# The order of the three partial products inside one half of a weight unit, in a one-core fp32 decoder step

## The reference, cut to what matters

```
z    = x @ w_in + b_in                      # 2048 x 6656: q, k, v, pooling input, two gates
d    = multi-scale causal pooling of z's pooling part
pool = (d @ w_pool[g]) * pool_scale         # 4 groups, 256 x 512 each
attn = sliding-window attention @ w_attn_br # 1024 x 2048
m    = sigmoid(g_pool) * pool + sigmoid(g_attn) * attn
h    = layer_norm(ALPHA * x + m @ w_out)    # 2048 x 2048
q    = h @ w_query                          # 2048 x 2048, then key scores and two top-16
a    = h @ peer_u.T                         # 16384 experts x 2048, computed for all experts here
y    = layer_norm(ALPHA * h + (gelu(a) * gate) @ peer_v)   # 16384 x 2048
```

## Time and profile before

| | |
|---|---|
| device time, median of 3 runs | 2319.65 us (2319.39 to 2319.66) |
| span of the profiled execution, first to last instruction | 2318.2 us |
| matmuls, and weight loads | 17575 and 17575 |
| TensorE busy (matmul) | 2301.9 us, 99% of the span |
| TensorE busy (weight load) | 2293.4 us |
| mean granted TensorE clock | 0.997 |
| VectorE, ScalarE, GpSimd busy | 1419.4, 882.9, 1702.8 us |
| read from and written to memory | 416.40 MB, 43.28 MB |

### The profile page before, as it was taken

One profiled execution on the slowest core, in us unless ns is written; L12 is line 12 of the kernel. 1 busy time (PEld: TensorE's weight loads), 2 busy tenths in 40 slices (PEclk: granted clock), 3 DMA queues, 4 the chain that ended last, 5 costly groups with the idle time before them and its releaser, 6 DMA issues.

```text
span 2318.2 us, 48204 instructions
## 1 busy us (share of the span) xinstructions
PE 2301.9 (99%) x17575; PEld 2293.4 (99%) x17575; DVE 1419.4 (61%) x2373; ACT 882.9 (38%) x1109; POOL 1702.8 (73%) x702
## 2 busy tenths in 40 slices
PE   9999999999999999999999999999999999999997
PEld 9999999999999999999999999999999999999997
DVE  3974564355569954656565640766666777666655
ACT  5444453345544443333333333333333333333334
POOL 4876677776677777677676767777777778777775
PEclk9999999999999999999999999999999999999998
DMA  7564446654455555666666668766666666666643
GB/s 255 168 200 146 145 143 206 213 173 154 146 164 194 185 191 184 217 215 211 211 209 213 208 216 257 282 205 206 209 215 220 217 213 206 208 206 217 199 164 114
DMA packets 141275, 458.25 MB, mean 198 GB/s; under 512 B 14448, under 2 KB 37232, under 8 KB 140656
## 3 DMA queue, kind: packets, MB, share of 16 engines
q1 hardware_dynamic: 116944, 416.42, 55.6%
q10 hardware_dynamic: 24264, 40.93, 4.8%
HBM read 416.40 MB, written 43.28 MB: 198 GB/s over the span
## 4 chain that ended last, share of the span: by engine, by line
PE 95%; DVE 4%; ACT 0%; issue 0%; ACTq 0%; DVEq 0%
PE ps L1412 30%; PE ps L1413 30%; PE ps L1418 30%; PE ps L1700 1%; DVE F L1010 1%; PE ps L1453 1%; DVE F L1011 1%; PE ps L1626 1%; PE ps L1645 0%; DVE b_lo L1024 0%; PE ps L1460 0%; DVE R L1039 0%; DVE R L1073 0%; PE ps L615 0%; ACT R L964 0%; PE ps L1551 0%
## 5 line engine op out<-in xcount | busy, mean ns | idle before, releaser
L707 POOL TENSOR_TENSOR w_lo<-raw,w_hi 128x1024 fp32r<-128x1024 f32 x692 | 1694.3, 2470 | 599.4 <-ACT w_hi L734 568.4
L734 ACT ACTIVATE w_hi<-raw 128x1024 fp32r<-128x1024 f32 x690 | 692.8, 1052 | 686.1 <-PE ps L1418 652.5
L1412 PE MATMUL ps<-a_hi,w_hi 128*128 128x288 f32 x3072 | 824.8, 295 | 0.0
L1413 PE MATMUL ps<-a_lo,w_hi 128*128 128x288 f32 x3072 | 822.6, 294 | 0.0
L1412 PE MATMUL ps<-b_hi,w_hi 128*128 128x288 f32 (+1 forms) x2432 | 655.1, 295 | 0.4 <-ACT w_hi L734 0.4
L1413 PE MATMUL ps<-b_lo,w_hi 128*128 128x288 f32 (+1 forms) x2432 | 653.0, 295 | 0.0
L1412 PEld LDWEIGHTS ps<-a_hi,w_hi 128*128 128x128 f32 x3072 | 577.7, 188 | 2.4 <-issue 2.2
L1413 PEld LDWEIGHTS ps<-a_lo,w_hi 128*128 128x128 f32 x3072 | 577.9, 188 | 0.1
L1418 PE MATMUL ps<-a_hi,w_lo 128*128 128x288 f32 x3072 | 467.2, 294 | 0.0
L1412 PEld LDWEIGHTS ps<-b_hi,w_hi 128*128 128x128 f32 x2432 | 457.1, 188 | 0.9 <-issue 0.8
L1413 PEld LDWEIGHTS ps<-b_lo,w_hi 128*128 128x128 f32 x2432 | 457.8, 188 | 0.1
(11 more groups left out here) (238 smaller groups left out, 1256.4 us busy)
## 6 DMA issues: line engine op xcount, KB each, us to landing
raw<-in_peer_u SPq DMA_DIRECT2D x256, 512.0 KB, 4.3
raw<-in_peer_v SPq DMA_DIRECT2D x256, 512.0 KB, 4.0
raw<-in_w_in SPq DMA_DIRECT2D x96, 512.0 KB, 3.9
gelu_scratch<-F ACTq DMA_DIRECT2D x32, 576.0 KB, 5.7
gate_scratch<-g_stage ACTq DMA_DIRECT2D x36, 512.0 KB, 6.0
F<-gelu_scratch SPq DMA_DIRECT2D x32, 576.0 KB, 5.7
raw<-in_w_out SPq DMA_DIRECT2D x32, 512.0 KB, 3.7
raw<-in_w_query SPq DMA_DIRECT2D x32, 512.0 KB, 3.7
```

What stands on the lines that cost most here:

```text
L707: pool.tensor_tensor(wl[:, j, s], raw[:, j, s], wh[:, j, s].bitcast(F32), ALU.subtract).then_inc(lo_ready, 1)
L734: act.activation(wh[:, k, s], raw[:, k, s], ACT.Copy).then_inc(hi_ready, 1)
L1412: pe.matmul(out, w, mh(k), start=(n == 0), stop=False)
L1413: pe.matmul(out, w, ml(k), start=False, stop=False)
```

## The change

`product` goes through the eight tiles of a half three times instead of twice: all high by high, then all high by low, then all low by high. The waits stay with the first pass over a half and with the low pass. The number of instructions stays the same.

```diff
                 for first in range(0, len(tiles), 8):
                     half = list(enumerate(tiles))[first:first + 8]
                     for n, (t, k) in half:
-                        w = wh[:, slot, t * P:t * P + P]
                         if t % 8 == 0:
 
                             pe.wait_ge(hi_ready, 2 * u + t // 8 + 1)
                         if m_wait:
 
                             pe.wait_ge(m_wait[0], m_wait[1] + n + 1)
-                        pe.matmul(out, w, mh(k), start=(n == 0), stop=False)
-                        pe.matmul(out, w, ml(k), start=False, stop=False)
+                        pe.matmul(out, wh[:, slot, t * P:t * P + P], mh(k), start=(n == 0), stop=False)
+                    for n, (t, k) in half:
+                        pe.matmul(out, wh[:, slot, t * P:t * P + P], ml(k), start=False, stop=False)
                     for n, (t, k) in half:
                         if t % 8 == 0:
```

## The result

The changed kernel takes 2326.94 us (median of 6 runs, 2326.79 to 2327.62), the kernel before 2319.63 beside it. The ratio is 1.0032, with a 95% interval of 1.0022 to 1.0042. So it is 7.3 us slower, where 2.3 us faster was forecast, and outside the range, which ended at 2322.0.

The account below looks back on a forecast made before the run. TensorE, busy 99% of the span with a load for every matmul, was taken as the bound. Gains of 0.3 + 0.9 + 1.1 = 2.3 us brought 2319.65 to 2317.4 us, range 2314.4 to 2322.0.

Parts of the forecast that it names:

- The a phases, 384 halves: Products reading a_hi and a_lo: 0.3 us less taken, bounds no gain and 1.2 us, near the low pass's 131.8 ns.
- The prediction's own sign of being wrong: Any half of 24 matmuls moving by over 6.8 ns, or a new wait for `hi_ready` or `lo_ready`.
- The third rival: Runs of successive high tiles fall on worse places: 0.007 us over 684 halves, 4.8 us slower, 2324.5; chance 0.06.
- attn and peer_v: 272 halves on `b`: 0.9 us less, from halves at 3.167 us coming to 3.160; bounds nothing and 2.2 us.
- a floor of 3.160: In peer_v, a half of 24 matmuls near 3.160 us was held to be the least possible.
- Query: 28 halves of 290 columns: from 3.24 to 3.200 us each, 1.1 us less; bounds 0 and 1.4.
- The waits: Only the first out unit's wait for its moving tiles shifts, still 1.5 us late enough: no cost.
- the fourth rival: Equal pairs share something, so each of 5504 L1413 loads gets dearer, up to 308 us, 2628; chance 0.02.
- The reuse of a loaded tile: Loading one weight once for two matmuls; the change would lose it, but the trace shows every matmul loading, so no cost.

## Why the prediction was wrong

**The step that failed** is "The a phases, 384 halves", where a low run's distance inside the alternating order was taken for what such a run would cost anywhere, with "no gain" as the lower bound. A loss was excluded with no ground. In the changed kernel the very same low runs, same tiles, same weights, take 133.1 in place of 131.8 ns. The term was −0.3 us; it measured +7.6. The distance of one matmul is not a property of its pass alone; the places of its neighbours set it too. The prediction's own sign of being wrong, a half that moves by over 6.8 ns, came up: the even halves moved by 48.

**The third rival was the one that came true**, with 6 chances in 100. Its mechanism (the order sets a pattern of places) is what the runs show; its price was off in both directions: it spread 7 ns over 684 halves, and in medians it was 48 and 5 ns on the even and odd halves of `a` (27 and 7 beside the gate sums). My argument against it, that good and bad halves follow each other with the low pass's mean, took the mean over one order as if it held for the next. The warning was on the table: halves that differ only in the slices read took 3.160 and 3.167, an effect of place, and I read it as a floor and not as a sign that I had no way of computing the term.

**attn and peer_v:** taken 0.9 us less, in peer_v; measured 0.0 over both. attn came down from 3.167 to 3.160, as was said of such halves. In peer_v the slower block came down to 3.160 and the faster one went up to 3.170, so "a floor of 3.160" was no rule.

**Query:** taken 1.1 us less; measured 0.2. The reference was `first_queries`, at 133.3 ns. In the changed kernel a low run of eight still takes (557.57 − 556.49)/8 = 135.0, as before:

```profile
556.49 1.24 PE L1418 MATMUL ps<-b_hi,w_lo 128*128 128x290 f32 x8
557.57 1.25 PE L1411 MATMUL ps<-b_hi,w_hi 128*128 128x290 f32 x8
```

`first_queries` has runs of 14 and no step back at tile 8. Whether that is why it is quicker was not tried.

**The waits** were right. In the changed kernel VectorE and TensorE at the start of the out phase:

```profile
431.16 0.46 DVE L1160 TENSOR_TENSOR a_lo<-ps,a_hi 128x288 f32 x1
```

```profile
429.02 1.22 PE L1411 MATMUL ps<-a_hi,w_hi 128*128 128x288 f32 x8
...
432.21 1.21 PE L1411 MATMUL ps<-a_hi,w_hi 128*128 128x288 f32 x8
```

The last tile is ready at 431.62 and wanted at 432.21 + 7 × 0.132 = 433.1: 1.5 us of cover, as worked out. Loads stayed at 188 to 189 ns and 17575, and the fourth rival's price is zero: 2432 new loads on `b` changed nothing. The reuse of a loaded tile, which the prediction weighed from the Trainium skill ("TensorE: Matmul & The Clock Gate", Step-by-step: what each phase is for), plays no part here.

**What stays open** is the mechanism below the rule. The rule is that, with three forward passes and tiles 1168 bytes apart, a run that begins at the weight tile's place modulo 256 bytes and follows a run over the same tiles is slow; the first run of the even half begins there too and is not. By how much it is slow, places and order do not settle: in the kernel with the weights moved, attn and the first block of peer_v that reads slices 8 to 15 take 3.240 us a half, and all later blocks of that kind, with the same places and the same order, 3.190. No run shows what makes this difference, nor whether beside the gate sums it is the sums on TensorE that change the halves. The Trainium skill ("TensorE: Matmul & The Clock Gate", Step-by-step: what each phase is for) says that weight loads and moving data have separate read ports, so that loading the next tile takes no read bandwidth from the running matmul. The runs do not agree that the two streams are independent: moving the weights by 64 bytes, while what the matmuls stream moved by 512, changed halves by −63 and +80 ns. Whether it is banks of the memory or something inside TensorE was not shown.

## What to carry to other kernels

In a stream of matmuls with no waits left, a reordering that changes no count can still move the time by some tenths of a per cent, up or down, through the operands' places in SBUF. Bound such a term on both sides, and not by the mean of one pass. The spread between stretches that differ in place alone is a better measure, but here it would still have been too small: 3.170 less 3.157 us, over 384 halves, is 5.0 us, and 7.6 were measured. Before keeping or dropping an order for 0.3%, try both orders at two or three places. Here a pad of 64 bytes under one operand was worth 9.0 us in its one run, more than the order, and with a pad of 192 bytes the order's effect turned its sign.

## What the runs showed of the hardware that was not expected

The distance between F32R matmuls of 288 columns in a row goes from 126 to 143 ns in a pattern that repeats from half to half, and averages 131.3 to 135.0 by half (3.150 to 3.240 us for 24). It depends on where the moving tile lies relative to the weight tile, modulo 256 bytes in the layouts tried, and on the order of tiles. Moving weights and operands together by 64 bytes changed nothing (2327.01 us against 2326.94), and VectorE's load did not matter where it was compared. Place and order are not all of it, as the 3.240 and 3.190 us above show. Tiles at exactly 1152 bytes (9 x 128) took 133.3 ns in either order, worse than most layouts with 1168.
